# Gathers of expert rows paced by TensorE's pieces, ten row buffers, one-hot spills issued by GpSimd

## What is computed

```python
q = (h @ wq).reshape(B, S, HEADS, 2, DHALF)
sub = einsum("bshpd,hpnd->bshpn", q, keys)      # scores of 128 keys, twice per head
sv, si = top_k(sub, 16)                          # both halves
best, pos = top_k(sv[...,0,:,None] + sv[...,1,None,:], 16)
experts = the 16 pairs (i, j) of key numbers, row number 128*i + j
gates = softmax(best)
act = gelu(einsum("cd,ced->ce", h, u_tab[experts]))   # 8 heads x 16 experts a token
out = einsum("ce,ced->cd", gates * act, v_tab[experts])
```

## Time and profile before

| | us |
|---|---|
| median of 3 runs | 1957.78 |
| lowest, highest | 1951.26, 1959.42 |
| the profiled execution's own time | 1952.49 |
| its span in the profile | 1950.7 |
| PE busy | 1862.3 (95%) |
| DVE busy | 1580.6 (81%) |
| ACT busy | 1031.1 (53%) |
| POOL busy | 783.9 (40%) |

### The profile page before, as it was taken

One profiled execution on the slowest core, in us unless ns is written; L12 is line 12 of the kernel. 1 busy time (PEld: TensorE's weight loads), 2 busy tenths in 40 slices (PEclk: granted clock), 3 DMA queues, 4 the chain that ended last, 5 costly groups with the idle time before them and its releaser, 6 DMA issues.

```text
span 1950.7 us, 34571 instructions
## 1 busy us (share of the span) xinstructions
PE 1862.3 (95%) x13106; PEld 1628.1 (83%) x13106; DVE 1580.6 (81%) x2510; ACT 1031.1 (53%) x1868; POOL 783.9 (40%) x686
## 2 busy tenths in 40 slices
PE   8999999999999999999998989988999999999997
PEld 7888887787889888788887877868999999998886
DVE  6768575676534999899987878878988999999998
ACT  5535454474555454666745656535674444444444
POOL 0000000000011113677635677004776777787773
PEclk9999999999999999999999999999999999999999
DMA  7523333246799997888868989977979999999997
GB/s 251 190 86 131 99 99 109 78 133 226 251 302 310 315 321 221 248 265 268 250 216 279 317 283 314 317 249 258 314 246 372 380 387 383 383 393 392 396 382 265
DMA packets 214741, 520.70 MB, mean 267 GB/s; under 512 B 25424, under 2 KB 98416, under 8 KB 214320
## 3 DMA queue, kind: packets, MB, share of 16 engines
q1 hardware_dynamic: 171952, 356.41, 52.9%
q0 software_dynamic: 42624, 162.08, 24.3%
HBM read 472.18 MB, written 46.20 MB: 266 GB/s over the span
## 4 chain that ended last, share of the span: by engine, by line
PE 60%; DMA 14%; DVE 14%; ACT 5%; issue 4%; POOL 3%; SPq 0%; DVEq 0%; ACTq 0%; POOLq 0%
PE ps L2043 59%; DVE lo L1330 4%; DMA raw<-in_peer_u 3%; DMA vraw<-in_peer_v 3%; DMA oneJ_spill<-hspace 2%; DMA hspace<-u_rows,row_ids 1%; POOL u_early L789 1%; PE ps L2447 1%; DMA u_late<-u_rows,row_ids 1%; ACT hi L870 1%; DMA u_early<-u_rows,row_ids 1%; POOL hspace L789 1%; POOL u_late L789 1%; DVE hspace L1862 1%; DMA oneI<-oneI_spill 1%
## 5 line engine op out<-in xcount | busy, mean ns | idle before, releaser
L2043 PE MATMUL ps<-hT,hi 128*128 128x512 f32 x2736 | 990.4, 405 | 39.1 <-DVE lo L1330 38.8
L2043 PE MATMUL ps<-hT,lo 128*128 128x256 f32 x2736 | 769.1, 281 | 0.0
L2043 PEld LDWEIGHTS ps<-hT,hi 128*128 128x128 f32 x2736 | 517.6, 189 | 176.3 <-issue 33.7
L870 ACT ACTIVATE hi<-raw 128x896 fp32r<-128x896 f32 (+1 forms) x406 | 397.2, 991 | 363.8 <-DMA raw<-in_peer_u 303.5
L1330 DVE TENSOR_TENSOR lo<-raw,hi 128x896 fp32r<-128x896 f32 (+1 forms) x406 | 457.6, 1139 | 126.8 <-ACT hi L870 122.5
L2043 PEld LDWEIGHTS ps<-hT,lo 128*128 128x128 f32 x2736 | 520.4, 190 | 0.1
L827 POOL DMA_INDIRECT got<-in_peer_v,row_ids x256 | 345.9, 1351 | 121.9 <-DVE sums L1338 100.9
L1203 ACT ACTIVATE vhi<-vraw 128x896 fp32r<-128x896 f32 (+1 forms) x256 | 193.6, 765 | 255.4 <-DMA vraw<-in_peer_v 247.7
L2043 PE MATMUL ps<-vhi,a_hi 128*128 128x448 f32 x768 | 242.0, 370 | 7.3 <-DVE vlo L1894 5.6
L1338 DVE SCALAR_TENSOR_TENSOR sums<-got,wT,sums 128x704 f32<-128x704 f32 x256 | 243.0, 949 | 1.4 <-DMA got<-in_peer_v,row_ids 0.9
L2043 PE MATMUL ps<-vlo,a_hi 128*128 128x448 f32 x768 | 241.0, 368 | 0.0
(11 more groups left out here) (314 smaller groups left out, 2257.2 us busy)
## 6 DMA issues: line engine op xcount, KB each, us to landing
raw<-in_peer_u SPq DMA_DIRECT2D x256, 448.0 KB, 4.8
vraw<-in_peer_v SPq DMA_DIRECT2D x124, 448.0 KB, 7.9
raw<-in_w_in SPq DMA_DIRECT2D x86, 512.0 KB, 3.4
vraw<-in_peer_v SPq DMA_DIRECT2D x124, 224.0 KB, 8.0
raw<-in_w_out SPq DMA_DIRECT2D x32, 512.0 KB, 3.8
raw<-in_wq SPq DMA_DIRECT2D x32, 512.0 KB, 5.3
turn_in<-in_peer_u SPq DMA_DIRECT2D x32, 512.0 KB, 5.9
u_rows<-turned POOLq DMA_DIRECT2D x32, 512.0 KB, 5.7
```

What stands on the lines that cost most here:

```text
L870: nc.scalar.activation(hi[n % NR][:, 0:w], raw[n % NR][:, 0:w], ACT.Copy).then_inc(hi_done, 1)
L2043: return nc.tensor.matmul(o, lhsT, rhs, start=start, stop=stop, skip_group_check=True)
```

## The change

- **Gathers.** GpSimd issues the first transfer of pair k when PE has finished all pieces up to the one 7 before that of its dot (`mm_done` at `DOT_AT[k] - LEAD`, LEAD = 6), and the second one piece later. It also waits for the dot of pair k - 6 (`dots_made`; the six landing semaphores are kept) and for the sum of the pair that used the same buffer last (`U_PREV`).
- **Buffers.** Ten instead of six: `hspace` 2 and `u_e` 8 in the first half, `hspace` 2, `u_l` 4 and `u_m` 4 in the second; from piece 196 on six, from piece 214 on four, since their place is then wanted for others.
- **Sums.** ACT sums a pair behind the `hi` of the piece three after that of its dot (SUM_LAG = 3), no longer by tiles.
- **Spills.** All spills of one-hots are issued by GpSimd. `pool_order` merges them with the gathers by the piece at which each is due; groups from `U_LATE` on follow behind all gathers. SP's queue has only loads in the U stage.
- **Late one-hots.** `U_LATE` is now the first group planned after the last dot, 35 instead of 47. J alternates between the buffer in `hspace` (two instructions) and a new one, `tail4`, in the unused ends of four `raw`/`hi` slots (one instruction), and DVE waits for the spill of the group two before.
- **Plan.** `pace` is 0.92 instead of 0.87: pairs 11 to 35 move up by one to two pieces. The last dot stays at piece 219.
- Two semaphores of the RWKV part are merged into one (`scan_steps`) with the same order of events.

```diff
-        pace = min(pace + 0.87, 2.0)
+        pace = min(pace + 0.92, 2.0)
...
-U_LATE = min([_i for _i, _n in ONE_AT.items() if _n >= 2 * (T_U + 117)] + [SEQ // 4])
+DOT_AT = {_i: _n for _n in U_STEPS for _what, _i in U_STEPS[_n] if _what == "dot"}
+U_LATE = min([_i for _i, _n in ONE_AT.items() if _n > LAST_DOT + 1] + [SEQ // 4])
+SUM_LAG = 3
+LEAD = 6
...
+    order, key = [], 0.0
+    for k in range(N_PAIR):
+        key = max(key, ROWS_AT[k * NT2 // N_PAIR], DOT_AT[k] - LEAD + 1,
+                  DOT_AT[k - U_BUF] + 0.6 if k >= U_BUF else 0)
+        order.append((key, k, "gather"))
+    order += [(ONE_AT[g] + 0.7, g, "spill") for g in range(U_LATE)]
+    return sorted(order)
...
             def made_j(g):
                 if g < U_LATE:
                     return madeJ[g % 3][:, :, :]
+                if (g - U_LATE) % 2:
+                    return tail4[:, :, 0:P]
                 return hspace[:, 0, 7:KC:8, :].rearrange("p a (b j) -> p a b j", b=2)
...
                 if k >= U_BUF:
-                    pool.wait_ge(sem("dots_summed"), k - U_BUF + 1)
+                    pool.wait_ge(sem("dots_made"), k - U_BUF + 1)
+                if U_PREV[k] is not None:
+                    pool.wait_ge(sem("dots_summed"), U_PREV[k] + 1)
...
                 for c in range(2):
+                    pool.wait_ge(mm_done, DOT_AT[k] - LEAD + c)
                     pool.indirect_dma_start(
...
+            for _, i, what in pool_order():
+                if what == "gather":
+                    gather_rows(i)
+                else:
+                    spill(i)
+            for g in range(U_LATE, N_TOK4):
+                spill(g)
...
-                if i < N_U - 1:
-                    hi_piece(2 * (T_U + i) + 2)
-                    hi_piece(2 * (T_U + i) + 3)
+                for n in range(2 * (T_U + i) + 2, 2 * (T_U + i) + 4):
+                    if n < 2 * T_V:
+                        hi_piece(n)
+                    for what, k in U_STEPS.get(n - SUM_LAG, []):
+                        if what == "dot":
+                            dots_sum(k)
...
-                if g > U_LATE:
-                    dve.wait_ge(sem(f"oneJ_out{(g - 1) % 3}"), 16 * ((g - 1) // 3 + 1))
-                elif 3 <= g < U_LATE:
+                if 3 <= g < U_LATE:
                     dve.wait_ge(sem(f"oneJ_out{g % 3}"), 16 * (g // 3))
+                if g >= U_LATE + 2:
+                    dve.wait_ge(sem(f"oneJ_out{(g - 2) % 3}"), 16 * ((g - 2) // 3 + 1))
```

## The result

The changed kernel takes **1964.39 us** (median of 16 runs) against 1957.57 for the kernel before (16 runs): ratio 1.0041, 95% interval 1.0024 to 1.0058. On another chip the same pair gave 1.0004 (0.9981 to 1.0027). So it is 0 to 0.4% slower, no difference by the prediction's own bound of 0.5%, where a gain of 11 us was forecast. The profiled execution took 1961.29 us with a span of 1959.5, which is 8.8 us above the span of before.

A forecast was written before the change was run, and what follows sets the result against it. PE was taken as the bound at 2.475 us a piece, with GpSimd's queue filling the middle. Terms -7 + 4 - 9 + 1 = -11 us gave 1946.8, say 1947 us; range 1925 to 1967.

The forecast's parts named there:

- The middle: Pieces 151 to 219: spills replace GpSimd's waits for sums, so GpSimd needs the whole stretch; +4 us, range -12 to +10.
- its 3 us: Middle stretch: allowance of about 3 us for waits for `madeI` in front of gathers, where group 0's one-hots come late.
- my own sum: GpSimd's work in the middle at the low spill price: 130.3 gathers, 27.8 issue, 33 spills, 191 us, no waits.
- two sums: GpSimd's work in the middle without waits: 191 us at 0.57 us a spill, 202 at 0.753.
- The likeliest case: Whole kernel: 1947 us, own range 1938 to 1955, chance 48%; its middle stretch takes 199.6 us.
- The long gathers: Middle stretch: two gathers took 4.71 us instead of 0.95; if they don't come back, 7.5 us less.
- The first stretch: Pairs 11 to 63, 800.5 to 1011.8 us: ten buffers, pacing and finer sums gain 7 us, bounds 0 and 10.8.
- The late part: Piece 219 to the stage's end: two J buffers make one-hot groups just fit; gain 9 us, bounds 1 and 12.9.
- The casts: Row-number casts for the next stage, behind GpSimd's last spill, some 5 us later: nothing, or +1 us if not hidden.
- GpSimd is not the bound: Rival, 17%: gathers get shorter in the middle, which gains 14 us; whole kernel about 1926 us.
- the late part gives nothing: Rival, 20%: GpSimd's late spills land after 5.6 us, so the second J buffer gains nothing; about 1955 us.
- Slower: GpSimd over its limit: Rival, 15%: spills cost 1.05 us each with issue, the middle takes 219 us; whole kernel about 1965 us.

The follow-up runs named there:

- Run 2: The changed kernel with the `u_m` buffers first used from pair 74 instead of 70, spills still on GpSimd: 1946.94 us, ratio 1.0016 to the kernel before.
- run 1: The changed kernel with all spills issued by SP again, at their old places between loads: 1922.43 us, ratio 0.9889 to the kernel before.
- run 6: The changed kernel with J's spills on SP and I's still on GpSimd: 1943.75 us, ratio 0.9886 to the kernel before.
- run 4: The kernel before with only the late part changed (earlier `U_LATE`, two late J buffers, spills on SP): 1935.78 us, ratio 0.9947.
- Run 7: The kernel before with only its spills moved to GpSimd, between the gathers: 1998.88 us, ratio 1.0161.
- run 8: The changed kernel with spills issued by ACT two pieces behind their one-hots, and `u_m` first used from pair 74: 1933.51 us, ratio 0.9824.
- run 9: One chip: kernel before 1961.76 us; change 1959.55; its gather part alone 1936.84; change with spills on SP 1928.21, with `u_m` also later 1924.73.
- run 3: The changed kernel with three I buffers before the late one-hots, `tail` serving as third J buffer: 1955.28 us, ratio 1.0061 to the kernel before.

## Why the prediction was wrong, point by point

- **The middle (+4 forecast, +18.8 measured) is the step that failed**, and it was called the one on which everything turns. The mechanism was seen: GpSimd's 33 us of waits are replaced by spills, and it needs as long as the stretch. The price of a spill was right too, 0.57 forecast, 0.583 measured and with no issue time of its own. Wrong were the counts, one wait that has no term at all, and the end of the argument:
  - 68 spills stand in the stretch, not 58. I counted groups 2 to 30 by the plan; groups 0 and 1 lag behind the wait for `idx`, and groups 31 to 33 belong to it as well. 10 x 0.58 = 5.8 us. Only the four of groups 0 and 1 held gathers; groups 31 to 33 were spilled behind the last gather, which ended at 1237.28, and 3.5 us of waits for DVE stand among them.
  - 114 gathers, not 108. The ones behind the first use of `u_m` slid into the stretch: 6 x (1.18 + 0.28) = 8.8 us. The wait is part of the change (the `bank_free` semaphores that stand ahead of pairs 72 and 73 in GpSimd's order stand ahead of pair 70 too), and the prediction has no term for it: its 3 us are for another wait, that of pair 73 for `madeI`, and the rows show none there (only 0.30 of issue before 1037.52). What it holds is not one pair but the whole queue.
  - With these my own sum gives 191 + 5.8 + 8.8 = 205.6, just what GpSimd's busy and issue time came to (174.1 + 31.7 = 205.8). The other 8.6 us are waits of GpSimd, 3.5 of them at the very end. PE waited for 7.18 us before 1041.28 because the first spills of I were late and DVE stood 9.0 us for `madeI`. Run 2 shows what the start was worth, some 5 us, runs 1 and 6 what the spills were, 25.1 and 11.9 us.
  - I took the middle of two sums that both assumed no wait at all, and 3 us more, as if an engine could be at 100% and the others lose nothing. The likeliest case should have lain above both sums.
- **The long gathers** of the earlier trace rows (-7.5 us if they stayed away) did stay away: no gather of `u_rows` took over 1.91 us in the change. So what the queue cost is more than the 18.8 us, by whatever these two had cost before. They are no accident of one trace: run 4, whose middle is that of before, has both again, 4.70 us at 1046.96 and 4.71 at 1151.07, against 1047.19 and 1151.41 in before. Run 7 has one of 3.69 and one of 3.08 us, run 8 one of 5.49, run 1 one of 2.16, and not in its repetition. What makes them stays open.
- **The first stretch**: -7 forecast, -4.4 measured (-3.8 in the repetition). DVE's waits for rows fell from 12.6 to 3.3 us in the two largest rows, so the mechanism holds. The size is not settled: for paced versions the stretch differs by 7.7 us between chips (202.8 to 210.5), and the kernel before was traced on one. What is left above the floor of 200.5 is not explained either: of PE's 4.2 us without work 3.7 are issue and 0.4 a wait for DVE.
- **The late part**: -9 forecast, -8.6 measured, inside 92 to 98 us. The J spills on the chain landed in 4.3 to 5.6 us, as the rows had it. With SP issuing them the same part took 92.9 us against 96.7 on one chip (run 9), so GpSimd had a small price here too. The chain of waits after:

```profile
1257.46 0.70 DVE tail L1903
1258.16 2.26 issue
1260.42 4.35 DMA oneJ_spill<-tail
1264.77 0.02 issue
1264.79 0.70 DVE tail L1903
1265.49 0.28 issue
1265.78 4.66 DMA oneJ_spill<-tail
```

- **The casts**: +1 forecast. From the end of the stage to the end of the span it is 619.2 us after and 619.5 before: nothing.
- **Pieces 144 to 151**: nothing forecast, +2.2 in the first trace of the change and -0.1 in the second.
- **The rivals.** "GpSimd is not the bound" and "the late part gives nothing" are refuted by the same rows. "Slower: GpSimd over its limit" had the right place and nearly the right length, 219 us, but by a price of 1.05 us a spill that isn't there: it was the count and the queue. Its own sign, over 210 us with direct transfers above 0.9, came half true: 214.4 us with 0.583.
- The range of 1925 to 1967 held the 1964.4 us, near its end; that is luck: the gains of the first stretch and the late part made up for most of what the middle lost.

## What to carry to other kernels

Before work is moved onto an engine's queue, add up what the queue then holds in that stretch, busy, issue and the waits that stay, and count its instructions in the changed order and not in the old plan; where the sum reaches the stretch's length, each microsecond more had a price of 0.60 and 0.63 here, and the likeliest result lies above the sum, not on it. In a queue that runs in order, a wait in front of one instruction is a wait for everything behind it: a first use of a buffer that is still being read belongs at a place where nothing urgent follows. And when a wait is cured by a buffer (run 3) and the time stays, look at how full the one is that releases it.

## What the runs showed of the hardware

- A spill issued by GpSimd in the middle took 0.577 to 0.591 us in the mean (0.589 and 0.621 in run 3) and had no issue gap when its one-hots were ready, while a gather had 0.30 before it, also behind a spill. From `hspace` in two runs a partition it took 0.678 us in the change's late part, from `tail` in four runs 0.721 there and 0.803 in the kernel of run 3 (11 of them). 256 KB and 128 KB took the same.
- Gathers took 1.09 to 1.28 us in the mean in the middle of all versions (by buffer), and 0.94 to 0.95 at the shortest, as in the timeline above. With spills between them the mean of all was 1.183 us in the change, against 1.206 in before, and the spills stayed at 0.58: what stretches most gathers did not stretch the spills in the same queue.
- The granted clock was at 0.50 in the window that follows 7.18 us without a matmul, and at 1.00 again in the one from 1050; the matmuls of 512 columns took 0.63 us until 1046 and 0.39 from 1047.05 on. The stretch's mean of 0.93 hides it; the same pieces took 5.9 us of PE's time more than in before.
